# First stage of a two-layer streaming encoder: modulation pairs regrouped, the first projection chunks run between them, one pair moved, cache transposes split

## The chip, the cores and the metric

The kernel runs on one core of a Trainium2 chip. The metric is the device time of one execution, in microseconds (us); smaller is better. PE is TensorE, DVE is VectorE, ACT is ScalarE, POOL is GpSimd, and SP is the engine whose queue issues most of the transfers from HBM.

## The reference

Two streams of frames (256 prompt frames, 64 frames of a running stream, side by side as 320 columns) pass through two layers of width 1024. What matters here is the beginning of a layer:

```
c_act = silu(c)
mod = c_act @ w_ada[l] + b_ada[l]                 # (1024) @ (1024, 6144)
shift_m, scale_m, gate_m, shift_f, scale_f, gate_f = split(mod, 6)
h = rmsnorm(x, g_norm_mix[l]) * (1 + scale_m) + shift_m
q, k, v, iq, ik, iw, glu, sc, gates = split(h @ w_in[l], offsets)
```

k and ik (64 columns each) are the attention keys and the indexer keys. The running stream has 512 cached keys, values and indexer keys and two short histories for convolutions; they are joined to the new ones. Sparse attention, a 31-tap convolution on `glu`, a 3-tap convolution on `sc`, gated merging, an output projection and a feed-forward part (dense in layer 0, eight experts in layer 1) follow. All of it is float32.

## The kernel before

Activations lie transposed: 1024 channels are 8 blocks of 128 partitions by 320 columns (`xT`, `hT`). Every engine has one program, written out by hand, and they meet at counting semaphores; each engine works in its own order, and so does each transfer queue.

**Weights** come through `ring`, four slots of 1 MB, numbered in one sequence by `plan()`. `load(n)` on SP waits until chunk n - 4 has been computed (`chunk_done`), so the order of numbers is the order on SP and on PE. `ring_lo` and `hT_lo` lie in the same memory as `ring` and `hT`: the low part is written in place over the value.

**Modulation.** The 6144 columns of `w_ada` are cut into 12 pairs of ring units, 512 columns each (`ADA_COLS`); a unit holds half of the 1024 rows. `ada_pair` multiplies (64 small matmuls), ACT copies the sum to `modrow` (`ada_evac`), PE transposes it (`ada_turn`), DVE (`mods_add`) or ACT (`mods_bias`) adds the bias and counts `mods_added`. In layer 0 the pairs 0 to 3 (`ADA_FIRST`) give shift_m and scale_m: pair 0 and 1 the eight blocks of the shift, pair 2 and 3 those of the scale. Pair 4 belongs to the gate.

**Norm.** ACT squares x, `norm_sums` adds over channels on PE with a matrix of ones, ACT takes the root (`norm_std`), DVE the reciprocal (`norm_stats`); `norm_apply` on DVE and `norm_scale` on ACT make `hT` block by block (`h_ready`). Then `hT_hi` (ACT, rounded) and `hT_lo` (DVE, the difference) are made.

**Order on PE at the start of layer 0:** transposes of x; pairs 0 and 1; `norm_sums(0)`; turns of 0 to 3 with pairs 2 and 3 between them; two plain float32 chunks for K and indexer K (`pair_chunk("qkv", l, 0)` and `1`, weights in ring slots, each loaded twice side by side to fill 128 columns); pair 4; and then the 27 split chunks of `SPLIT`, of which the first are glu 0, glu 1, qkv 2, qkv 4 (v and indexer weights, 72 columns), qkv 3. A split chunk is three matmuls for each pair of blocks: high weight by high h, high weight by low h, low weight by high h. ACT makes the high part of a chunk's weights in two halves (`mix_high(s, r)`) and DVE the low part (`mix_low(s, r)`), both two chunks ahead: in its step s ACT does `mix_high(s + 2, 0)`, which waits until the load has landed, then the evacuation of chunk s, then `mix_high(s + 2, 1)`. The code between the two halves of a chunk on PE is the function `between`.

**Caches.** SP issues 14 small transfers (`cache_loads`) behind the load of glu 1. Behind chunk 2 (`S_CACHE`) PE turns them in seven batches through three banks of PSUM (`cache_transposes`), and DVE copies each out (`cache_copies`, counting `cache_copied`); the fourth batch can start only when the first is copied. POOL waits for all seven before it forms `u_conf`, which the convolution taps on DVE (`conv_taps`, dealt out over the steps by `TAPS_AT`) read. In the middle of chunk 4 (`S_KV`) PE turns the keys (`kv_transposes`), and waits there for `cache_copied` 7:

```
pe.wait_ge(mods_added, ADA_PAIRS * l + ADA_AT_QKV[l][1] + 1)
if l == 0:
    pe.wait_ge(cache_copied, 7)
pe.wait_ge(pair_evac, pair_no["qkv", l, 4] + 1)
```

The order on DVE in a step s is `mix_low(s + 2, 0)`, taps, `mix_low(s + 2, 1)`, `cache_copies` where it has its place, taps.

Of the kernel before, what the change touches and what calls it, by code (L numbers as in the profile page):

```python
# [27 lines left out]
P = 128  # L28
# [60 lines left out]
ADA_AT_QKV = ({1: 4}, {1: 6})  # L89
# [26 lines left out]
def plan():  # L116
# [17 lines left out]
    for l in range(DEPTH):  # L134
        for j in range(2):
            chunk("qkv", l, j)
            if j in ADA_AT_QKV[l]:
                ada(l, ADA_AT_QKV[l][j])
        for s, (stage, j) in enumerate(SPLIT[:NPROJ]):
            chunk(stage, l, j)  # L140
            if s in ADA_AT_SPLIT[l]:
                for h in range(2):
                    side[l, 2 * ADA_AT_SPLIT[l][s] + h] = len(side)
# [23 lines left out]
def build(nc, x_prompt, x_sample, cache_k, cache_v, cache_idx_k, state_conv_conformer, state_conv_short,  # L167
# [6 lines left out]
    with ExitStack() as ctx:  # L174
# [185 lines left out]

        sq_mix = wide[:, 0:DC, :]
# [44 lines left out]
        x_loaded = sem("x_loaded")  # L406
        caches_loaded = sem("caches_loaded")
# [165 lines left out]
        def _(sp):  # L573
# [26 lines left out]
            def ada_loads(l, m):  # L600
                for h in range(2):
                    parts = halves(ada_rows(l, 2 * m + h),
                                   w3["ada"][l][:, 4 * h:4 * h + 4, ADA_COLS * m:ADA_COLS * (m + 1)], 4)
# [13 lines left out]
            for m in range(ADA_FIRST):  # L617
                ada_loads(0, m)

# [11 lines left out]
            for l in range(DEPTH):  # L631
                win = w3["in"][l]
                for i, c in enumerate((K0, IK0)):
                    n = ring_no["qkv", l, i]
                    v = slot_view(n % SLOTS, DC, P)
                    load(n, [(v[:, :, r * HD:(r + 1) * HD], win[:, :, c:c + HD]) for r in range(2)])
                    if i in ADA_AT_QKV[l]:
                        ada_loads(l, ADA_AT_QKV[l][i])
# [4 lines left out]
                for s, (stage, j) in enumerate(SPLIT[:NPROJ]):  # L643
# [13 lines left out]
                    else:  # L657
# [3 lines left out]
                        if l and j == 8:  # L661
                            sp.wait_ge(mods_added, DEPTH * ADA_PAIRS)
                            for s_ in range(2):
                                for c in range(DC):
                                    sp.dma_start(gate_dram[s_, c * P:(c + 1) * P].unsqueeze(1),
                                                 mods[:, l, 40 + c, s_:s_ + 1]).then_inc(gate_stored, 16)
                    if s == 1 and l == 0:
# [90 lines left out]
        def _(pool):  # L758
# [14 lines left out]
            for l in range(DEPTH):  # L773

                pool.wait_ge(cache_copied, 7)
# [47 lines left out]
        def _(pe):  # L823
# [133 lines left out]
            def cache_transposes():  # L957
# [3 lines left out]
                for n in range(7):  # L961
                    b = (lg[:, 0:512], lg[:, 512:1024], px)[n % 3]
                    if n >= 3:
# [16 lines left out]

            pe.wait_ge(c_ready, 1)
            ada_pair(0, 0)
            ada_pair(0, 1)
            norm_sums(0)
            for m in range(ADA_FIRST):
                ada_turn(0, m)
                if m + 2 < ADA_FIRST:
                    ada_pair(0, m + 2)


            for l in range(DEPTH):
# [4 lines left out]
                pair_chunk("qkv", l, 0, h_rhs, blocks=((0, P),), width=P, each=h_each(2 * l))  # L996
                pair_chunk("qkv", l, 1, h_rhs, blocks=((0, P),), width=P)
# [1352 lines left out]
```

## Time and profile before

| | |
|---|---|
| median of 3 runs | 1468.35 us (1465.03 to 1468.79) |
| the profiled execution, its own time | 1463.33 us |
| its span in the trace | 1461.6 us |
| PE busy | 1391.8 us, 95% of the span |
| DVE busy | 1023.0 us, 70% |
| ACT busy | 781.2 us, 53% |
| POOL busy | 42.1 us, 3% |
| mean granted clock of PE | 0.981 of full speed |

The span is what the trace shows from the first to the last instruction; 1.7 us of the execution's time lie around it. A granted clock of 1.00 is 2.4 GHz, one of 0.50 is 1.2 GHz. The three runs differ among themselves by 3.8 us, and the profiled execution was faster than all of them.

### The profile page before, as it was taken

The page shows a single profiled execution, that of the slowest core. Times are in us where ns is not written, and L with a number is a line of the kernel's source. Part 1 is how long each engine was busy: PE and PEld are TensorE (multiplying, and loading weights), DVE is VectorE, ACT ScalarE, POOL GpSimd, SP SyncE. Part 2 cuts the span into 40 slices and gives each one's busy share as a digit, 9 for nine tenths or more (in the row PEclk, how much of TensorE's full clock was granted, in tenths as well). Part 3 has the DMA queues.
Part 4 walks back from the last instruction along what each step waited for, and adds up shares of the span by engine and source line. Part 5 has one row for each costly group of instructions (what it writes and reads, how often), then busy time and mean ns, then how long its engine had stood idle before and what let it go on. Part 6 is the DMA issues. An engine that isn't in the chain of part 4 may idle for free.

```text
span 1461.6 us, 24398 instructions
## 1 busy us (share of the span) xinstructions
PE 1391.8 (95%) x9311; PEld 1227.0 (84%) x9311; DVE 1023.0 (70%) x1401; ACT 781.2 (53%) x1058; POOL 42.1 (3%) x66
## 2 busy tenths in 40 slices
PE   5899999999889999997999999999799999999996
PEld 4788999877789999996989998778488888888884
DVE  2376999875554444235678998754788988898886
ACT  2534448634433333224444486344677887788763
POOL 0010100000000000000001000000200000000010
PEclk8999999999989999999999999999899999999999
DMA  9956744224546867543667764244689999999993
GB/s 305 244 165 194 258 133 131 73 72 149 167 137 195 259 201 238 200 129 96 209 202 252 213 139 151 73 136 159 247 303 386 386 381 384 376 386 386 377 381 115
DMA packets 282691, 328.40 MB, mean 225 GB/s; under 512 B 34654, under 2 KB 192806, under 8 KB 282598
## 3 DMA queue, kind: packets, MB, share of 16 engines
q1 hardware_dynamic: 276146, 317.18, 66.1%
q0 software_dynamic: 1472, 5.24, 1.0%
q10 hardware_dynamic: 4980, 4.69, 0.9%
q8 instruction: 63, 1.03, 0.3%
q14 instruction: 30, 0.25, 0.1%
HBM read 312.41 MB, written 14.66 MB: 224 GB/s over the span
## 4 chain that ended last, share of the span: by engine, by line
PE 89%; DVE 4%; DMA 3%; ACT 2%; SPq 1%; issue 1%; POOLq 0%; POOL 0%; DVEq 0%; ACTq 0%
PE mmp L856 14%; PE mmp L858 14%; PE mmp L857 14%; PE mmp L1258 8%; PE mmp L1260 8%; PE mmp L1259 8%; PE mmp L850 8%; PE py L826 2%; PE px L906 2%; DMA ring<-in_w_ada_dram 2%; PE lg L1022 1%; PE px L1064 1%; PE lg L906 1%; PE py L922 1%; DMA y_late<-rows_dram,pos_i 1%
## 5 line engine op out<-in xcount | busy, mean ns | idle before, releaser
L856 PE MATMUL mmp<-hT_hi,wm_hi 128*128 128x320 f32 (+1 forms) x976 | 306.7, 314 | 6.5 <-issue 4.9
L858 PE MATMUL mmp<-hT_hi,ring_lo 128*128 128x320 f32 (+1 forms) x976 | 304.3, 312 | 0.0
L857 PE MATMUL mmp<-hT_lo,wm_hi 128*128 128x320 f32 (+1 forms) x848 | 262.7, 310 | 0.0
L1867 DVE TENSOR_TENSOR ring_lo<-ring,wm_hi 128x1024 fp32r<-128x1024 f32 (+1 forms) x124 | 148.3, 1200 | 79.7 <-ACT wm_hi L1456 76.0
L856 PEld LDWEIGHTS mmp<-hT_hi,wm_hi 128*128 128x128 f32 (+1 forms) x976 | 183.1, 188 | 11.0 <-issue 7.3
L858 PEld LDWEIGHTS mmp<-hT_hi,ring_lo 128*128 128x128 f32 (+1 forms) x976 | 182.8, 187 | 0.2
L1456 ACT CAST wm_hi<-ring 128x1024 fp32r<-128x1024 f32 (+1 forms) x124 | 126.7, 1029 | 94.5 <-PE mmp L858 71.5
L857 PEld LDWEIGHTS mmp<-hT_lo,wm_hi 128*128 128x128 f32 (+1 forms) x848 | 159.0, 187 | 0.1
L1413 ACT ACTIVATE tmp<-mmp 128x320 f32<-128x320 f32 x70 | 30.6, 438 | 215.7 <-PE mmp L858 163.4
L1955 DVE SCALAR_TENSOR_TENSOR conv<-u_conf,dwc,conv 128x350 f32<-128x350 f32 x240 | 132.1, 581 | 3.0
L2089 DVE TENSOR_TENSOR wd_lo<-ring,wd_hi 128x2048 fp32r<-128x2048 f32 (+1 forms) x34 | 75.7, 2229 | 64.0 <-ACT wd_hi L1621 63.8
L856 PE MATMUL mmp<-h_hi,wd_hi 128*128 128x320 f32 x352 | 111.4, 316 | 8.8 <-DVE h_lo L2113 8.8
L857 PE MATMUL mmp<-h_lo,wd_hi 128*128 128x320 f32 x352 | 109.9, 312 | 0.0
L858 PE MATMUL mmp<-h_hi,wd_lo 128*128 128x320 f32 x352 | 109.9, 312 | 0.0
L2159 DVE TENSOR_TENSOR more_lo<-more,we_hi_a 128x2048 fp32r<-128x2048 f32 (+1 forms) x48 | 92.1, 1934 | 21.8 <-ACT we_hi_a L1674 19.0
L1258 PE MATMUL mmp<-we_hi_a,xg_hi 128*128 128x512 f32 (+1 forms) x256 | 98.4, 384 | 2.4 <-DVE xg_lo L2221 2.4
L2159 DVE TENSOR_TENSOR more_lo<-more,we_hi_b 128x2048 fp32r<-128x2048 f32 (+2 forms) x48 | 92.0, 1930 | 8.6 <-ACT we_hi_b L1674 8.6
L1260 PE MATMUL mmp<-we_hi_a,xg_lo 128*128 128x512 f32 (+1 forms) x256 | 97.2, 380 | 0.0
L2159 DVE TENSOR_TENSOR ring_lo<-ring,we_hi_a 128x2048 fp32r<-128x2048 f32 (+2 forms) x48 | 91.8, 1930 | 7.0 <-ACT we_hi_a L1674 6.9
L1621 ACT CAST wd_hi<-ring 128x2048 fp32r<-128x2048 f32 (+1 forms) x34 | 62.9, 1852 | 56.9 <-PE mmp L858 29.3
L1674 ACT CAST we_hi_a<-ring 128x2048 fp32r<-128x2048 f32 (+2 forms) x48 | 77.1, 1620 | 20.0 <-PE mmp L1260 15.5
L1674 ACT CAST we_hi_b<-more 128x2048 fp32r<-128x2048 f32 (+2 forms) x48 | 77.7, 1619 | 8.9 <-ACT y L1741 4.4
(389 smaller groups left out, 2851.8 us busy)
## 6 DMA issues: line engine op xcount, KB each, us to landing
ring<-in_w_in_dram SPq DMA_DIRECT2D x104, 512.0 KB, 4.9
ring<-in_w_exp_in_dram SPq DMA_DIRECT2D x64, 512.0 KB, 8.5
more<-in_w_exp_in_dram SPq DMA_DIRECT2D x64, 512.0 KB, 11.3
ring<-in_w_ada_dram SPq DMA_DIRECT2D x56, 512.0 KB, 6.8
more<-in_w_exp_out_dram SPq DMA_DIRECT2D x48, 512.0 KB, 6.1
ring<-in_w_ffn_in_dram SPq DMA_DIRECT2D x44, 512.0 KB, 5.8
wide<-in_w_ada_dram SPq DMA_DIRECT2D x40, 512.0 KB, 7.6
ring<-in_w_branch_dram SPq DMA_DIRECT2D x48, 256.0 KB, 2.9
```

Of the source, the lines that this page charges most:

```text
L850: ins = nc.tensor.matmul(mmp[0:m, 2 * (q % 2) + b, 0:T], v[:, i, c0:c0 + m], rhs(i), start=(i == 0), stop=(i == k - 1))
L856: nc.tensor.matmul(out, w_hi, x_hi, start=is_first, stop=False)
L857: nc.tensor.matmul(out, w_hi, x_lo, start=False, stop=False)
L858: return nc.tensor.matmul(out, w_lo, x_hi, start=False, stop=is_last)
L1258: nc.tensor.matmul(bank, x_hi, w_hi, start=is_first, stop=False)
L1259: nc.tensor.matmul(bank, x_hi, w_lo, start=False, stop=False)
L1260: return nc.tensor.matmul(bank, x_lo, w_hi, start=False, stop=is_last)
L1456: copy(mix_hi(l, s, r), mix_rows(ring, l, s, r)).then_inc(mix_hi_ready, 1)
L1674: copy(we_hi(k)[:, 0:sizes[kk]], we_raw(k)[:, 0:sizes[kk]]).then_inc(hi_ready, 1)
L1867: V.tensor_tensor(mix_rows(ring_lo, l, s, r), mix_rows(ring, l, s, r), mix_hi(l, s, r).bitcast(F32), ALU.subtract).then_inc(mix_lo_ready, 1)
L1955: ins = V.scalar_tensor_tensor(conv[:, c, :], src, tap, conv[:, c, :], ALU.mult, ALU.add)
L2159: V.tensor_tensor(we_lo(k)[:, 0:size], we_raw(k)[:, 0:size], we_hi(k)[:, 0:size].bitcast(F32), ALU.subtract).then_inc(lo_ready, 1)
```

## The change

Layer 0 alone changes, apart from renamed constants.

- **Pairs 0 to 3** now hold two blocks of shift and the two matching blocks of scale each. Their transfers read two stretches of 256 columns (rows of 1 KB) where they read one of 512 (rows of 2 KB). `mods_add` becomes two additions, `gains` and `norm_apply` run for two blocks after each pair.
- **PE** does `norm_sums(0)` first, then each pair with its turn at once behind it, and after each of the turns 1, 2, 3 and once more at the end the K and indexer K products of two blocks of h (`keys_first`).
- **K weights** no longer use the ring. They are loaded once, into the unused `merged`, between pair 1 and pair 2 on SP's queue, and ACT doubles them side by side.
- **ACT** scales two blocks of h after each pair and rounds them; **DVE** makes the low parts as soon as `keys_first` has read a block.
- **Pair 4** is loaded and computed behind glu 1; its turn stands in the middle of qkv 2.
- **Cache transposes and copies** come in two portions: batches 0 to 2 behind chunk 2, batches 3 to 6 behind chunk 3, the last through another bank. POOL waits for three in layer 0.

```diff
-ADA_AT_QKV = ({1: 4}, {1: 6})
+ADA_AT_QKV = (4, 6)
+ADA_BEHIND = (1, None)
...
-        ring[stage, l, j], pair[stage, l, j] = n, q
-        n, q = n + 1, q + 1
+        pair[stage, l, j] = q
+        q += 1
+        if (stage, l) != ("qkv", 0) or j >= 2:
+            ring[stage, l, j] = n
+            n += 1
...
         for s, (stage, j) in enumerate(SPLIT[:NPROJ]):
             chunk(stage, l, j)
+            if s == ADA_BEHIND[l]:
+                ada(l, ADA_AT_QKV[l])
...
+                    v, src = ada_rows(l, 2 * m + h), w3["ada"][l][:, 4 * h:4 * h + 4, :]
+                    if m < ADA_FIRST:
+                        parts = [(v[:, :, 2 * P * r:2 * P * (r + 1)],
+                                  src[:, :, D * r + 2 * P * m:D * r + 2 * P * (m + 1)]) for r in range(2)]
...
             for m in range(ADA_FIRST):
                 ada_loads(0, m)
+                if m == 1:
+                    for i, c in enumerate((K0, IK0)):
+                        sp.dma_start(wk0[:, i, :, 0:HD], w3["in"][0][:, :, c:c + HD]).then_inc(k_loaded, 16)
...
+                    if s == ADA_BEHIND[l]:
+                        ada_loads(l, ADA_AT_QKV[l])
                     if s == 1 and l == 0:
                         cache_loads()
...
-                pool.wait_ge(cache_copied, 7)
+                pool.wait_ge(cache_copied, (3, 7)[l])
...
+            def keys_first(m):
+
+                if m == 0:
+                    pe.wait_ge(k_doubled, 2)
+                for c in range(2 * m, 2 * m + 2):
+                    pe.wait_ge(h_ready, c + 1)
+                    for j in range(2):
+                        ins = nc.tensor.matmul(mmp[:, 2 * (pair_no["qkv", 0, j] % 2), 0:T], wk0[:, j, c, :], hT[:, c, :],
+                                               start=(c == 0), stop=(c == DC - 1))
+                ins.then_inc(k_done, 1)
+
+            norm_sums(0)
             pe.wait_ge(c_ready, 1)
             ada_pair(0, 0)
+            ada_turn(0, 0)
             ada_pair(0, 1)
-            norm_sums(0)
+            ada_turn(0, 1)
             for m in range(ADA_FIRST):
-                ada_turn(0, m)
+                keys_first(m)
                 if m + 2 < ADA_FIRST:
                     ada_pair(0, m + 2)
+                    ada_turn(0, m + 2)
...
                     def between():
+                        if ADA_BEHIND[l] is not None and s - 1 == ADA_BEHIND[l]:
+                            ada_turn(l, ADA_AT_QKV[l])
...
+                    if s == ADA_BEHIND[l]:
+                        ada_pair(l, ADA_AT_QKV[l])
                     if s == S_CACHE and l == 0:
-                        pe.wait_ge(mods_added, ADA_AT_QKV[0][1] + 1)
-                        cache_transposes()
+                        pe.wait_ge(mods_added, ADA_AT_QKV[0] + 1)
+                        cache_transposes(range(3))
+                    if s == S_CACHE + 1 and l == 0:
+                        cache_transposes(range(3, 7))
...
                     norm_std(0)
-                    for m in range(2, ADA_FIRST):
+                    for m in range(ADA_FIRST):
                         ada_evac(0, m)
-                    norm_scale(0, gain_of(0), shift_of(0))
+                        if m == 1:
+                            act.wait_ge(k_loaded, 32)
+                            for j in range(2):
+                                copy(wk0[:, j, :, HD:P], wk0[:, j, :, 0:HD]).then_inc(k_doubled, 1)
+                        if m >= 1:
+                            norm_scale(0, gain_of(0), shift_of(0), range(2 * m - 2, 2 * m))
+                            high_h(range(2 * m - 2, 2 * m))
+                    norm_scale(0, gain_of(0), shift_of(0), range(DC - 2, DC))
+                    high_h(range(DC - 2, DC))
...
+                if l == 0:
+                    mix_high(0, 0)
...
+                    if ADA_BEHIND[l] is not None and s - 1 == ADA_BEHIND[l]:
+                        mods_bias(l, ADA_AT_QKV[l])
...
+                    if s == ADA_BEHIND[l]:
+                        ada_evac(l, ADA_AT_QKV[l])
...
                     for m in range(ADA_FIRST):
                         mods_add(0, m)
-                    gains(0, 0)
-                norm_apply(2 * l)
+                        gains(0, 0, 2 * m, 2 * m + 2)
+                        norm_apply(0, 2 * m, 2 * m + 2)
+                        if m == ADA_FIRST - 2:
+                            hT_lows(range(DC // 2))
...
                     if s == S_CACHE and l == 0:
-                        cache_copies()
+                        cache_copies(range(3))
+                    if s == S_CACHE + 1 and l == 0:
+                        cache_copies(range(3, 7))
```

## Rows read from the trace of the kernel before

**Rows 1.** The page, part 1: busy us, share of the span, instructions.

```profile
PE 1391.8 (95%) x9311; PEld 1227.0 (84%) x9311; DVE 1023.0 (70%) x1401; ACT 781.2 (53%) x1058; POOL 42.1 (3%) x66
```

**Rows 2.** Timeline of PE, 0 to 80 us: start us, us, instructions, idle before.

```profile
14.18 0.63 PE L941 MATMUL mmp<-ident,wide 96*128 96x96 f32 x2 [2.64 <-DMA wide<-in_w_dw_conf_dram]
...
20.29 4.57 PE L922 MATMUL py<-wide,ones 128*128 128x320 f32 x16
...
24.91 1.95 PE L906 MATMUL px<-ring,c 128*32 128x128 f32 x64
...
33.39 0.48 PE L915 MATMUL lg<-ident,modrow 128*128 128x128 f32 x1
36.54 11.13 PE L850 MATMUL mmp<-hT,ring 128*128 128x320 f32 x32 [2.67 <-ACT hT L1389]
...
52.61 0.39 PE L856 MATMUL mmp<-hT_hi,wm_hi 128*128 128x320 f32 x1 [3.06 <-issue]
...
75.51 1.03 PE L972 MATMUL lg<-ident,wide 128*128 128x128 f32 x8
```

**Rows 3.** Timeline of DVE and ACT before K.

```profile
25.54 2.15 DVE L1831 RECIPROCAL rstd<-std 128x320 f32<-128x320 f32 x1 [10.11 <-ACT std L1382]
...
35.79 4.84 ACT L1389 ACTIVATE hT<-hT,mods,gain 128x256 f32<-128x256 f32 x8 [2.45 <-DVE hT L1843]
```

**Rows 4.** Windows of 1 us: length, PE busy, granted clock, DMA share, GB/s.

```profile
13.00:14.00 1.00, 0.00 (x0) 0.92 1.04 333
...
17.00:18.00 1.00, 1.00 (x40) 0.87 1.03 332
...
23.00:24.00 1.00, 1.00 (x5) 1.00 0.99 365
...
31.00:32.00 1.00, 0.98 (x20) 0.50 1.33 220
...
69.00:70.00 1.00, 1.00 (x9) 1.00 1.09 382
...
79.00:80.00 1.00, 0.45 (x2) 0.50 1.19 298
...
85.00:86.00 1.00, 1.00 (x7) 0.74 0.00 0
```

**Rows 5.** Timeline of SP's queue.

```profile
43.40 5.30 SPq L588 DMA_DIRECT2D ring<-in_w_in_dram  x4
...
58.51 30.16 SPq L588 DMA_DIRECT2D ring<-in_w_in_dram  x12
```

**Rows 6.** Landing of the transfers issued from 59.6 us (qkv 4).

```profile
DMA to landing us min/median/max: 6.5/6.8/7.1
```

**Rows 7.** Landing of one issued at 75.7 us with nothing ahead.

```profile
DMA to landing us min/median/max: 4.0/4.0/4.0
```

**Rows 8.** Waits, 0 to 110 us: total, times, longest.

```profile
PE mmp L856 <- ACTq L1416: 1.3, 1, 1.3
...
PE lg L972 <- DVE kTs L1809: 2.4, 1, 2.4
```

**Rows 9.** Timeline of DVE, 45 to 150 us.

```profile
78.81 0.68 DVE L1809 COPY kTs<-lg 128x512 f32<-128x512 f32 x1
...
80.01 0.28 DVE L1811 COPY hist<-px 128x128 f32<-128x128 f32 x1
...
83.34 0.29 DVE L1807 COPY dwc<-lg 128x124 f32<-128x124 f32 x1
85.37 1.01 DVE L1952 TENSOR_SCALAR conv<-u_conf,dwc,vec 128x350 f32<-128x350 f32 x1 [1.74 <-POOL u_conf L788]
...
90.53 2.18 DVE L1955 SCALAR_TENSOR_TENSOR conv<-u_conf,dwc,conv 128x350 f32<-128x350 f32 x4
...
93.89 3.30 DVE L1955 SCALAR_TENSOR_TENSOR conv<-u_conf,dwc,conv 128x350 f32<-128x350 f32 x6
```

**Rows 10.** The chain that ended last: the key transposes in chunk 4.

```profile
91.24 0.57 PE lg L1009 x6
```

More of the change, by code:

```diff
@@ L633, in _ @@
                 for i, c in enumerate((K0, IK0)):
[L634 to L638, printed above, removed]
+                    if l:
+                        n = ring_no["qkv", l, i]
+                        v = slot_view(n % SLOTS, DC, P)
+                        load(n, [(v[:, :, r * HD:(r + 1) * HD], win[:, :, c:c + HD]) for r in range(2)])
+                if ADA_BEHIND[l] is None:
+                    ada_loads(l, ADA_AT_QKV[l])
                 def clear_rows(b):
@@ L1383, in norm_std, with norm_scale @@
                                      bias=eps[:, 0:1]).then_inc(std_ready, 1)
-            def norm_scale(k, gain_of, shift_of):
-                for c in range(DC):
+            def norm_scale(k, gain_of, shift_of, blocks=range(DC)):
+                for c in blocks:
                     act.wait_ge(xn_ready, DC * k + c + 1)
@@ L1423, in shift_of, with high_h @@
                     return lambda c: mods[:, l, 24 * which + c, 0:1]
+                def high_h(blocks):
+                    for c in blocks:
+                        act.wait_ge(h_ready, DC * 2 * l + c + 1)
+                        copy(hT_hi[:, c, :], hT[:, c, :]).then_inc(hT_hi_ready, 1)
                 if l == 0:
@@ L1436, in _ @@
                     norm(2 * l, gain_of(0), shift_of(0))
[L1439 to L1446 removed]
+                    high_h(range(DC))
                 def mix_high(s, r):
@@ L1456, in mix_high @@
                     copy(mix_hi(l, s, r), mix_rows(ring, l, s, r)).then_inc(mix_hi_ready, 1)
-                for r in range(2):
+                if l == 0:
+                    mix_high(0, 0)
+                for j, (dst, dst_s) in enumerate(((kT, kTs), (ikT, ikTs))):
+                    if l:
+                        chunk_wait(ring_no["qkv", l, j])
+                    else:
+                        act.wait_ge(k_done, ADA_FIRST)
+                    copy(dst[:, 0:T], pair("qkv", l, j, 0))
+                    copy(dst[:, T:TW], pair("qkv", l, j, 0)[:, TP:T])
+                    copy(dst_s[:, l, PAST:NKS], pair("qkv", l, j, 0)[:, TP:T]).then_inc(pair_evac, 1)
+                for r in range(2) if l else (1,):
                     mix_high(0, r)
-                ada_evac(l, ADA_AT_QKV[l][1])
+                if ADA_BEHIND[l] is None:
+                    ada_evac(l, ADA_AT_QKV[l])
                 for r in range(2):
@@ L1798, in _, with cache_copies @@
             link(V.tensor_copy(dwc[:, 0, :], mmp[:, b % 4, P:P + CW * BC]))
-            def cache_copies():
-                for n in range(7):
-                    s = (lg[:, 0:512], lg[:, 512:1024], px)[n % 3]
+            def cache_copies(batches):
+                for n in batches:
+                    s = (lg[:, 0:512], lg[:, 512:1024], px)[n % 3] if n < 6 else py
                     l, what = n // 3, n % 3
```

119 lines of the change are left out of this document (70 added, 49 removed).

## The prediction

> **What bounds the kernel now.** The page first: PE is busy for 1391.8 of 1461.6 us [rows 1]. A change pays only where it shortens PE's own way through the program. Next the granted clock in windows of 1 us, because everything here happens in the first 91 us, where PE has pauses: it falls to half in the pause before 14 us, is back at 17.9, is at half again from 31 to about 41, and once more from 79 to 85.7 [rows 4]. Then the timelines. PE starts glu 0, the first split chunk, at 52.61, the transposes of the caches at 75.51, and the key transposes in the middle of chunk 4 at 91.24 [rows 2, 10]. From there PE has no gap, and nothing behind it is changed. So the question is only when PE reaches the key transposes, and at what clock. I call these times G (start of glu 0), E (end of qkv 2) and V (key transposes): before, G = 52.6, E = 75.5, V = 91.2.
>
> **G, the part that gains.** I follow the new order from the last unchanged moment, the small transposes at 14.18 [rows 2], which end at 14.8.
>
> - The channel sums come first: 4.57 us at full clock [rows 2]. The clock is half until 17.9 [rows 4], so 3.1 us do 1.6 us of the work, and the sums end at 20.9.
> - Pair 0 takes 1.95 us [rows 2] to 22.8. Now its turn follows at once. Pair 3's turn starts at 33.39, 0.4 us after its last matmul (1.94 us from 31.02), for ACT's copy between. So each pair with its turn costs 1.95 + 0.4 + 0.3 = 2.65, and pair 1 is turned at 25.8. The reciprocal of 2.15 us [rows 3] lies beside this.
> - The first products of K need both doublings of the weights (my estimate 0.6 us each, between ACT's 0.43 us for 320 columns and 1.05 for 1024) and one scaled block (eight in 4.84 us, and PE starts 0.75 after the first begins [rows 2, 3]): 25.2 + 0.3 + 1.2 + 0.75 = 27.5.
> - The 32 matmuls of K took 11.13 us partly at half clock [rows 2]; at full clock one starts each 0.27 us, eight are 2.15 us. From 27.5: K 29.7; pair 2 has landed by 30.1 and is done at 31.5, turned at 32.2; K again needs a block scaled after pair 2's copy, 32.6 to 34.8; pair 3 to 36.7, turn 37.4; K 37.8 to 40.0, and 40.0 to 42.1.
> - Landing: a unit of 1.05 MB takes 2.9 us at 365 GB/s [rows 4]. K's 0.5 MB, in rows of 256 bytes, goes at 220 GB/s [rows 4], 2.4 us, ahead of pair 2. And pair 2's load waits until pair 0 is computed, now 5 us later than before, so the queue runs dry for some 2 us. First unit free at 21.8, then 5.5 to land, then 2.9 each: 27.3, 30.2, 33.1, 36.0. PE asks for the last at 35.75: no more than 0.3 us is lost.
> - Then ACT's cast and DVE's difference for glu 0 (1.05 and 1.23 us) start at 41.3, behind the rounding of the last block. glu 0's weights are there: their slot is free at 30.6. Before, their load was issued at 43.40 [rows 5], and PE's start hung on it. G = 43.7.
>
> With one fall of the clock after the pause of 25.8 to 27.5 (before, pauses like it cost the clock at 14 and at 31, but a longer one at 50 did not) some 4.5 us run at half, 2.2 us of loss. At an even chance that is 1.1. G = 44.8, **7.8 us earlier**. Bounds: 41 (below) and 48 (two falls).
>
> **G to E, the part that gives back.** Three chunks take 75.51 - 52.61 less the 1.3 us of waiting for ACT [rows 2, 8]: 7.2 each. Now pair 4 stands between glu 1 and qkv 2: +1.95. The wait of 1.3 goes (qkv 2's load was issued at 58.51, behind the cache transfers [rows 5]; now it goes out at G + 7.3, lands by G + 12.3, and ACT frees the bank by G + 15.5, before PE needs it at 16.4).
>
> But the turn of pair 4 stands in the middle of qkv 2, at G + 14.4 + 1.95 + 3.6 = G + 19.95, and needs ACT's `ada_evac`, which stands behind `mix_high(3, 0)`, the evacuation of glu 1 and `mix_high(3, 1)`. `mix_high(3, 0)` waits for the load of qkv 4. That load takes the slot of glu 1, so it is issued at G + 14.5, two transfers 0.5 apart; from issue to landing they took 6.5 to 7.1 us behind other transfers [rows 6], and one with nothing ahead took 4.0 [rows 7]. I take 5.3: landed at G + 20.3. ACT then needs 2.0 us for the four steps (read from the same steps at 69.97 to 71.95). The turn is at G + 22.4, PE has stood for 2.4 us (1.1 with 4.0, 4.2 with 7.1), and qkv 2 ends at 22.4 + 0.3 + 3.6 = G + 26.3. Before it was G + 22.9: **+3.4**. A pause of that length may take the clock; at an even chance half of 3.6 us, **+0.9**. qkv 3's load is queued behind qkv 4's, ACT's bias for pair 4 behind the cast of qkv 3, and PE asks for that bias before the transposes: 0 to 1.5, I take **+0.5**.
>
> **E to V, the split of the caches.** It takes away PE's wait of 2.4 us for the fourth batch [rows 8]; the half clock that follows on it (to 85.7) goes too. On PE alone E to V would shrink from 15.7 to about 10.2: 1.2 for three batches, 3.6 for chunk 3, 1.8 for four batches, 3.6 for half of chunk 4. But PE still waits for `cache_copied` 7 there, and on DVE the last four copies now stand behind step 3's taps and `mix_low(5, 1)`. DVE's chain from E: the first copy began 3.3 after E [rows 2, 9] (evacuation, cast, difference); three copies 1.5, to the end of the third [rows 9]; POOL's `u_conf`, which DVE waited 1.74 for [rows 9]; six taps, `mix_low(5, 0)`, four taps, `mix_low(5, 1)`: 93.89 - 85.37 = 8.5 [rows 9]; four copies, 1.5 for three and 0.5 for the two small ones; 0.1 for the semaphore. 3.3 + 1.5 + 1.7 + 8.5 + 2.0 + 0.1 = 17.1, where it was 15.7: **+1.4**. PE stands for about 7 us in the middle of chunk 4. Before, it had got back its full clock at 85.7, ahead of V; now the clock has certainly fallen and comes back 3.7 (from 14.2) to 6.1 us (from 79.6) after PE resumes [rows 4], a loss of half: 1.8 to 3.0, I take **+2.3**. Behind V DVE is ahead by its six taps, which nobody waits for; the first side load, which waits for the seven transposes, is earlier by more than it needs.
>
> **Nothing for** the second addition in `mods_add` and the gains in four portions (0.2 us each, beside PE's pairs), SP's 14 cache issues (9.8 us, now in glu 0's shadow; without that cover qkv 2's load would slip by up to 6), and the last batch in another bank.
>
> **Rows of 1 KB.** The first pairs are read in rows half as long. In this trace such rows, those of qkv 3, moved at 382 GB/s, the present 2 KB rows at 365 [rows 4]: no cost. The Trainium skill ("DMA: Bandwidth & Descriptors", Why small descriptors are slow) puts a fixed 3 cycles on every packet beside one for each 32 bytes, 35 for 32 against 67 for 64, which would be 4.5% on 8.4 MB, an estimate of 1.0 us later at the last pair. By that rule the sum would be up to 1 us higher; by the rows it is not.
>
> **The sum**: -7.8 + 3.4 + 0.9 + 0.5 + 1.4 + 2.3 = +0.7 us. Against the profiled execution: 1463.3 + 0.7 = 1464.0. That execution lies 5.0 below the median, so the median would be 1469.0.
>
> **Rivals.**
> 1. *The early stage runs at full clock.* If w_dw_conf's rows, for which PE stood until 14.18 [rows 2], arrive with the first squares (13.1), the clock does not fall, the sums end at about 16.5, pair 2 is loaded without a dry queue, and G is 41.0 to 41.5 by the transfers alone (9.7 MB at 365 GB/s and K's 2.4 us, less 2.8 at the last pair). With no fall after it and the short landing of qkv 4: -3.6 - 1.3 - 0.9 more, a sum of about -5, 1463. For it: 1 KB rows leave the other queue more often a turn. Against: the sums and squares are unchanged, and 333 GB/s flowed without pause. The Trainium skill (same page, Queues, rings and completion order) has engines change queues at whole packets, of several rows each; if so, shorter rows give the small transfers nothing, and this rival loses its ground.
> 2. *The chain on DVE does not bind.* If PE walks through E to V at its own 10.2 us, the last two terms become -5.5 and 0: -8.5, 1460. For it only that four copies are 2 us of work. It decides if the copies are done by E + 10; the order on DVE says E + 17.
> 3. *Slower: half clock between the pairs.* PE's work from 27.5 to 42.1 is 12.5 us in short pieces with pauses for ACT between. If the clock stays at half there, as it did from 31 to 41 [rows 4], these are 25, of which pauses and landings cover 3 to 4: G near 53, sum +9, 1477. From 10 us at half clock on it is slower by more than 0.3%. For it: before, the same stage did run so. Against: PE was idle for half of it, now for a fifth.
>
> **Chances.** 0.3% is 4.4 us, about what runs of this kernel (3.8 us apart) can tell from no change. The forecast, within that: 0.58. Rival 1: 0.15, rival 2: 0.07, both faster, 0.22. Rival 3 and its milder forms: 0.20. The range leaves out rival 2 and the upper part of rival 3: from -7.4 to +6.7, 1461 to 1475.
>
> **What would show it.** G at 43 to 46. PE waiting at its turn in the middle of qkv 2 for ACT, 1 to 4 us. DVE's last four copies behind the difference of chunk 5, and PE idle some 7 us before the key transposes, which start at about 89, then half clock for 4 to 6 us. It is wrong if the key transposes start before 85, if PE does not stand there, or if K's products run at 0.53 us each.

## The result and the profile after

The changed kernel takes 1470.86 us (median of 20 runs, 1465.68 to 1476.26) against 1466.02 for the kernel before in the same comparison (20 runs, 1460.58 to 1474.29). The ratio is 1.0024, 95% interval 1.0013 to 1.0034: 3.5 us slower, between 1.9 and 5.0. (The ratio is that of the means; the medians lie 4.8 us apart.) The 3.5 us are inside the 0.3% which the prediction called no change, near its upper edge. A second comparison (12 and 23 runs) gave 1.0036 [1.0015, 1.0058]. The forecast was 1469.0 us and +0.7. It starts from a median of 1468.3 for the kernel before, where this comparison has 1466.0, so the +0.7 is the number to judge: its sign is right and its size too small.

| profiled execution | before | after |
|---|---|---|
| own time, us | 1463.33 | 1466.45 |
| span, us | 1461.6 | 1464.7 |
| G, start of glu 0 | 52.61 | 45.01 |
| E, end of qkv 2 | 75.51 | 72.30 |
| V, key transposes | 91.08 | 89.40 |
| S, first scores of the attention | 95.60 | 96.73 |

(V of before is the start on PE's timeline. The chain of [rows 10] enters that group at 91.24, the moment from which the prediction counted its 15.7.) I add S, the first matmul of `lg<-prob,iqT`, because part of the price of a pause is paid behind V.

The page after, part 1, answers to [rows 1]:

```profile
PE 1394.1 (95%) x9311; PEld 1227.3 (84%) x9311; DVE 1025.3 (70%) x1415; ACT 782.1 (53%) x1060; POOL 44.3 (3%) x66
```

PE does the same number of matmuls and is busy 2.3 us longer: the added time is not all waiting, some of it is work at a lower clock.

**The early stage.** Timeline of PE of the changed kernel, 12 to 64 us, beside [rows 2]:

```profile
13.08 0.41 PE L968 MATMUL mmp<-ident,wide 96*128 96x96 f32 x2 [1.88 <-DMA wide<-in_w_dw_conf_dram]
13.33 6.16 PE L949 MATMUL py<-wide,ones 128*128 128x320 f32 x16
19.42 1.95 PE L933 MATMUL lg<-ring,c 128*32 128x128 f32 x64
...
26.09 3.52 PE L1015 MATMUL mmp<-hT,merged 128*128 128x320 f32 x8 [1.30 <-ACT hT L1437]
...
32.93 2.42 PE L1015 MATMUL mmp<-hT,merged 128*128 128x320 f32 x8 [0.17 <-ACT hT L1437]
...
37.09 1.08 PE L933 MATMUL lg<-ring,c 128*32 128x128 f32 x32 [0.72 <-DMA ring<-in_w_ada_dram]
...
39.10 4.88 PE L1015 MATMUL mmp<-hT,merged 128*128 128x320 f32 x16 [0.17 <-ACT hT L1437]
45.01 0.39 PE L883 MATMUL mmp<-hT_hi,wm_hi 128*128 128x320 f32 x1 [1.04 <-ACT kTs L1517]
...
59.26 1.95 PE L933 MATMUL px<-ring,c 128*32 128x128 f32 x64
63.51 0.42 PE L883 MATMUL mmp<-hT_hi,wm_hi 128*128 128x320 f32 x1 [2.30 <-ACTq L1464]
```

Each line can be laid beside the walk in the prediction. A pair with its turn takes 2.65 us, as forecast (the next pair starts at 22.07). The first eight products of K are slow, 3.52 us, and the next eight take their 2.42 us at full clock. The wait of 1.04 before glu 0 is put down to ACT's copy of the keys, but that was done at 44.67. What PE waited for longest is DVE's difference for glu 0, which ends at 44.91, as the prediction had it.

**The clock in that stage**, windows of 1 us of the changed kernel. The columns are length, busy us (and instructions) of PE, PEld, DVE, ACT and POOL, then the granted clock, the DMA share and GB/s:

```profile
13.00:14.00 1.00, 0.92 (x4) 0.78 (x5) 0.44 (x2) 1.00 (x3) 0.00 (x0) 0.78 1.10 346
16.00:17.00 1.00, 1.00 (x3) 0.61 (x3) 0.00 (x0) 0.00 (x0) 0.00 (x0) 0.52 1.11 351
21.00:22.00 1.00, 0.56 (x17) 0.24 (x5) 1.00 (x1) 0.27 (x1) 0.00 (x0) 1.00 0.50 110
27.00:28.00 1.00, 1.00 (x4) 0.70 (x3) 0.00 (x0) 0.15 (x1) 0.00 (x0) 0.60 1.05 368
```

The clock fell at about 13.6, and once more behind the pause at 26, to half from about 27.2 to 30.6; then no more before glu 0. In [rows 4] the kernel before ran at half here from 31 to 41. The queue ran dry at 21 to 22 us (110 GB/s), as forecast.

**The caches.** Timeline of DVE of the changed kernel, 74 to 92 us, beside [rows 9]:

```profile
74.46 1.22 DVE L1958 TENSOR_TENSOR ring_lo<-ring,wm_hi 128x1024 fp32r<-128x1024 f32 x1 [3.23 <-ACT wm_hi L1506]
75.60 0.68 DVE L1875 COPY kTs<-lg 128x512 f32<-128x512 f32 x1
...
76.80 0.28 DVE L1877 COPY hist<-px 128x128 f32<-128x128 f32 x1
78.82 1.00 DVE L2040 TENSOR_SCALAR conv<-u_conf,dwc,vec 128x350 f32<-128x350 f32 x1 [1.74 <-POOL u_conf L815]
...
80.61 2.19 DVE L2043 SCALAR_TENSOR_TENSOR conv<-u_conf,dwc,conv 128x350 f32<-128x350 f32 x4
82.83 1.23 DVE L1958 TENSOR_TENSOR ring_lo<-ring,wm_hi 128x1024 fp32r<-128x1024 f32 x1
83.97 2.18 DVE L2043 SCALAR_TENSOR_TENSOR conv<-u_conf,dwc,conv 128x350 f32<-128x350 f32 x4
86.19 1.23 DVE L1958 TENSOR_TENSOR ring_lo<-ring,wm_hi 128x1024 fp32r<-128x1024 f32 x1
87.33 0.69 DVE L1875 COPY kTs<-lg 128x512 f32<-128x512 f32 x1
...
89.01 0.29 DVE L1873 COPY dwc<-py 128x124 f32<-128x124 f32 x1
```

And what PE does meanwhile, in the chain that ended last:

```profile
77.57 0.87 PE lg L999 x8
82.90 6.50 issue
89.40 1.33 PE lg L1051 x6
```

The transposes of the fourth batch begin on PE at about 77.4 (the chain joins them at 77.57), and their copy on DVE at 87.33, ten us later, because the four copies, 2 us together, stand behind ten taps and two differences. "Issue" is the name for a wait that the profile connects with nothing; the releaser is the last copy, which ends 0.1 us before PE's first key transpose. The clock beside it:

```profile
85.00:86.00 1.00, 0.00 (x0) 0.00 (x0) 0.96 (x3) 0.00 (x0) 0.00 (x0) 0.62 1.06 403
...
95.00:96.00 1.00, 1.00 (x7) 1.00 (x6) 0.96 (x3) 0.00 (x0) 0.00 (x0) 0.76 0.38 82
```

It falls in the pause (0.62 in the slice from 85, so at about 85.2, 2.3 us after PE stopped) and is back at 95.5, 6.1 us after PE resumed. From V to S it takes 7.3 us, before 4.5.

### The profile page after: what moved, and what is told of

It is laid out like the page before. It is cut to its first block, busy times and chain, and to the rows that moved or that the text cites. A ratio compares the mean times of both kernels' runs of the same rounds, so it can differ in the third digit from the quotient of the medians.

```text
span 1464.7 us, 24425 instructions
## 1 busy us (share of the span) xinstructions
PE 1394.1 (95%) x9311; PEld 1227.3 (84%) x9311; DVE 1025.3 (70%) x1415; ACT 782.1 (53%) x1060; POOL 44.3 (3%) x66
## 4 chain that ended last, share of the span: by engine, by line
PE 87%; DVE 4%; DMA 2%; ACT 2%; SPq 2%; issue 1%; ACTq 0%; POOLq 0%; POOL 0%; DVEq 0%
PE mmp L883 13%; PE mmp L885 13%; PE mmp L884 13%; PE mmp L1306 8%; PE mmp L1308 8%; PE mmp L1307 8%; PE mmp L877 7%; PE px L933 2%; PE py L853 2%; DMA ring<-in_w_in_dram 1%; PE py L949 1%; PE lg L1064 1%; PE lg L933 1%; SPq L690 1%; PE px L1106 1%
## 5 line engine op out<-in xcount | busy, mean ns | idle before, releaser
L1461 ACT ACTIVATE tmp<-mmp 128x320 f32<-128x320 f32 x70 | 30.6, 437 | 213.9 <-PE mmp L885 161.7
L2179 DVE TENSOR_TENSOR wd_lo<-ring,wd_hi 128x2048 fp32r<-128x2048 f32 (+1 forms) x34 | 75.7, 2230 | 65.0 <-ACT wd_hi L1687 64.9
```

## The experiments

All results are ratios to the kernel before on the same chip, with 95% intervals, unless us are named. "In its trace" is one execution. First the two parts of the change were separated.

**One portion.** The changed kernel with caches turned and copied as before:

```diff
-                        cache_transposes(range(3))
-                    if s == S_CACHE + 1 and l == 0:
-                        cache_transposes(range(3, 7))
+                        cache_transposes(range(7))
```

and the same for `cache_copies`; POOL waits for seven again, and the last batch is in its old bank.

> The changed kernel with the cache transposes and copies in one portion again (seven batches behind chunk 2, POOL waiting for seven, the last batch in its old bank); all else as changed. My theory (what the split costs: DVE's last four copies lie behind ten taps, PE stands in the middle of chunk 4 and then runs at half clock): PE's wait of 6.5 us before the key transposes goes, one of about 2.4 us for the fourth batch returns, E to V is 15.7 us instead of 17.1, and the clock is full at V. That is 4 us less than the changed kernel, a ratio of 0.999 to 1.000 to the kernel before. Rival (the loss comes from somewhere else, the split costs nothing in the end): 1.002 to 1.003 as the changed kernel.

Measured: 0.999 [0.997, 1.001]. In its trace E to V is 14.6 (changed kernel 17.1) and V to S 4.5 (7.3). So everything but the split is worth 1.5 us of gain, with an interval from a gain of 4.4 to a loss of 1.5, and the split costs the changed kernel some 5 us (0.999 against 1.0024; from the two intervals, an estimate of 5 with 3 either way).

**The split alone.** The kernel before, with the two portions of the diff and nothing else of it.

> The kernel before with the split of the cache transposes and copies alone. My theory: E stays at 75.5, V comes at E + 17.1 = 92.6 instead of 91.2, PE stands some 6 us in the middle of chunk 4 and runs at half clock for some 5 us behind it: 1.4 + 2.9, slower by 4 us, a ratio of 1.002 to 1.004. Rival (the split does what it does on PE alone: it removes the wait of 2.4 us and the half clock that follows): V at 86 to 88, faster by 3 to 5 us, 0.997.

Measured: 1.0040 [1.0026, 1.0055], 5.9 us slower (3.8 to 8.1). In its trace E to V is 17.1, PE idles 6.50 us ahead of V, and V to S is 7.2. It is the same picture without any of the other edits:

```profile
90.30 6.50 issue
96.79 1.33 PE lg L1009 x6
```

**The four copies ahead of the taps.** The changed kernel, where DVE's order alone differs; PE's order stays (excerpt, as all edits here):

```diff
                     if s == S_CACHE and l == 0:
                         cache_copies(range(3))
-                    if s == S_CACHE + 1 and l == 0:
                         cache_copies(range(3, 7))
```

> The changed kernel, split kept on PE, but DVE does its last four cache copies right behind the first three, ahead of the six taps that end step 2. My theory: PE reaches the key transposes by its own work, about 10.2 us behind the end of qkv 2, without the wait of 6.5 us and without the half clock after it: 6.9 + 2.9 = 9.8 us less than the changed kernel, a ratio of 0.995 to 0.997 to the kernel before. Rival (the taps, now 1.5 us later, hold up the low parts of chunks 5 and 6, and PE waits there instead): PE idle at chunk 5 or 6, ratio 0.999 or more.

Measured: 0.9942 [0.9923, 0.9961], median 1459.89, more gain than the 0.995 to 0.997 expected: this one and "both", below, are the fastest kernels here. Timeline of DVE in its trace:

```profile
76.83 0.69 DVE L1875 COPY kTs<-lg 128x512 f32<-128x512 f32 x1 [0.97 <-PE lg L999]
...
78.52 0.29 DVE L1873 COPY dwc<-py 128x124 f32<-128x124 f32 x1
78.72 0.83 DVE L2040 TENSOR_SCALAR conv<-u_conf,dwc,vec 128x350 f32<-128x350 f32 x2
```

DVE waits 0.97 us for PE instead of 1.74 for POOL, and PE does not stand anywhere from E to V: 10.5 us, the "own 10.2" of the prediction. V is at 81.53 and S at 86.05. One line of order is worth 12 us (0.9942 against 1.0024).

**The four copies at the head of step 3**, behind step 2's taps only:

```diff
+                    if s == S_CACHE + 1 and l == 0:
+                        cache_copies(range(3, 7))
                     if s + 2 < NPROJ:
                         mix_low(s + 2, 0)
...
-                    if s == S_CACHE + 1 and l == 0:
-                        cache_copies(range(3, 7))
```

> The changed kernel, DVE's last four cache copies at the beginning of its step 3: behind the six taps that end step 2, ahead of the low part of chunk 5 and the four taps. A dose between the changed kernel (V at E + 17.1) and copies ahead of all taps (E + 10.3). My theory, the order on DVE alone: V at E + 12.6, PE waits about 2.4 us before the key transposes, too short to be sure that the clock falls: 4.5 to 7.4 us less than the changed kernel, a ratio of 0.996 to 0.999 to the kernel before. Rival (any pause there costs the clock, the place matters little): 0.999 to 1.001.

Measured: 0.9988 [0.9972, 1.0003]. E to V is 12.6, and V to S is 4.5. In the chain of its trace:

```profile
82.37 1.99 issue
84.36 0.76 PE lg L1051 x6
```

In this trace a pause of 2 us costs its 2 us and no clock; the one of 6.5 costs 2.2 to 2.8 more behind it in every trace that has it.

**The kernel before with the split, copies ahead of the taps.**

> The kernel before with the split of the cache transposes, and DVE's last four copies right behind the first three, ahead of the taps; nothing regrouped. My theory: the split done in this order removes the wait of 2.4 us for the fourth batch and the half clock that follows it: V at E + 10.4 instead of E + 15.6, 5 us less than the kernel before, a ratio of 0.996 to 0.998. If so, more than half of the gain of the changed kernel with this order (0.9942) comes from the caches and less than half from the pairs. Rival (the pause only moves, as it did in the changed kernel): 0.999 or more.

Measured: 0.9983 [0.9960, 1.0006], less gain than the expected 0.996 to 0.998. E to V is 10.4, as expected. With the split alone it was 1.0040, so the place of the four copies is worth 8.4 us in this kernel. Of the 8.5 us that the changed kernel gains with this order, 2.5 come from the caches (0.9983) and 6.0 from the rest of the change (0.9983 against 0.9942, some 4 us either way by the two intervals); more than half from the caches was expected.

**Pair 4 at the front**, behind pair 3 as before, in the changed kernel: `ADA_BEHIND = (None, None)`.

> The changed kernel with pair 4 loaded and computed in front of glu 0 again, split kept. My theory: G is 1.5 to 2.5 us later, but qkv 2's slot is free before glu 0 starts and the cache transfers are issued earlier, so PE waits neither at the start of qkv 2 nor at a turn in its middle: three chunks in 21.6 us instead of 27.3. E 3 to 4 us earlier, V at E + 17.1 as before: about 4 us less than the changed kernel, 0.9985 to 1.001 to the kernel before. Rival (moving pair 4 is worth its 1.95 us: it leaves the way to G and costs nothing behind): slower than the changed kernel, 1.003 or more.

Measured: 1.0016 [0.9997, 1.0036], outside the expected 0.9985 to 1.001. G moves to 48.8 and E stays, 72.2 against 72.3; G to E is 23.4 where 21.6 was expected. The start of glu 0 in PE's timeline:

```profile
48.81 0.39 PE L883 MATMUL mmp<-hT_hi,wm_hi 128*128 128x320 f32 x1 [2.24 <-ACT ikTs L1517]
```

Another 1.81 us go at the start of qkv 2. In front, PE waits 2.24 + 1.81 us at the two starts; with the pair behind glu 1 it is 1.04 + 2.30. E is 72.2 and 72.0 in the two traces with the pair in front, and 71.7 on the mean of the six with it behind and the caches on SP's queue: the place of the pair makes no difference that these runs can show.

**Regrouped pairs alone**: one portion and pair 4 in front.

> The regrouped pairs with K between them alone: caches in one portion, pair 4 in front of glu 0, as in the kernel before. My theory: G at 46 to 47 (52.6 before), E at G + 21.6 = 68, V at E + 15.7 = 84, full clock at V: 7 us earlier than before, a ratio of 0.994 to 0.997. Rival (the gain at G is lost again in E to V, or by half clock between the pairs, whatever the other parts do): 0.998 or more.

Measured: 0.9988 [0.9972, 1.0004], less gain than the expected 0.994 to 0.997. In its trace the clock fell around pair 3 (its second half took 1.93 us where 1.08 is usual), G was 49.4 and S 92.3, 3.3 ahead of the kernel before. With the caches in one portion the fourth batch waits 2.42 us again, and E to V is 15.8. The lead at S is there, and 1.8 us of it are in the time.

**Cache transfers on ACT's queue.** In the changed kernel the cost of SP's 14 issues was under suspicion (next section). They go out on ACT's queue behind `row_loads(1)`; the loop over the caches is the same, with `act.dma_start` for `sp.dma_start`.

> The changed kernel with the 14 cache transfers issued from ACT's queue behind the bias rows of layer 1, not from SP's ahead of qkv 2. In the changed kernel qkv 2's load is issued at 54.77 behind them, 2.7 us after glu 0 has ended. My theory: the load goes out at about 52.3, PE's wait of 2.3 us at the start of qkv 2 goes, but the turn of pair 4 in its middle waits for ACT instead, 0.5 to 2 us; E is 1 to 3 us earlier and everything behind it, as E to V stays 17.1: 1 to 4 us less than the changed kernel, 0.9995 to 1.002 to the kernel before. Rival (small transfers on a second queue slow qkv 2's load as much as the issues did): no difference, 1.0024.

Measured: 1.0032 [1.0016, 1.0047], where 0.9995 to 1.002 was expected. Its trace shows the mechanism that was expected: PE waits 0.92 us before qkv 2 and 0.47 at the turn, V is at 85.50 and S at 92.36, 4.4 earlier than in the changed kernel's first trace and 3.7 earlier than the mean of its three. On ACT's queue the 14 issues take 7.1 us. The time shows nothing of the lead: the mean granted clock is 0.9777 over its 12 runs and 0.9795 over the 29 of before beside them, and 0.0018 of the time is 2.6 us.

**Both: copies ahead and transfers on ACT's queue.**

> Two edits together on the changed kernel: DVE's last four cache copies ahead of the taps, and the cache transfers issued from ACT's queue. Alone they gave 0.9942 and 1.0032 to the kernel before. If the 4 us that the second one gained up to the key transposes in its trace are real and only lost in the scatter, this is 0.991 to 0.993. If ACT's issues give nothing in the end: 0.994 as the first alone.

Measured: 0.9943 [0.9924, 0.9963]. S is at 83.62, again 2.4 earlier than with the copies ahead alone, and again the time is the same. But the intervals of the two leave room for some 4 us either way, so this pair cannot tell 2.4 from nothing; the pair before it, with 4.4 us at S, is the one that speaks.

**Controls.** The changed kernel once more, timed; one more execution of the kernel before and one of the changed kernel, on the same chip.

> The changed kernel itself, once more beside the kernel before, on the chip of this call. It measures how much of the differences between my experiments is scatter between calls. Expected 1.001 to 1.004 (1.0024 so far), G at 44 to 46, V at E + 17.1. If the trace shows a fall of the clock near 885 and near 1050 us too, as seven of the eight experiments did and the two first traces did not, these falls belong to the chip or the execution and not to an edit.

> One look at the kernel before, for its trace alone. In the first trace the split chunks began at 52.6 us and the first scores at 95.6; with the same code up to there, the trace of the split alone began them at 55.8. Expected 52.5 to 56, and between 1366 and 1372 us from the first scores to the end. If it lies near 55.8, the first trace was an early one and the changed kernel's gain at G was larger than the 7.6 us that the two traces show.

> One look at the changed kernel, for its trace alone. Expected G at 44 to 46, the wait before the key transposes 6.5 us, and 1368 to 1376 us from the first scores to the end.

Measured: 1.0036 [1.0015, 1.0058] for the first; 1469.93 us for the one execution of before, 1475.06 for the last. Some expectations were missed at their edges: G of the changed kernel was 43.4 and 46.7 where 44 to 46 was expected, and span less S was 1377.0 in the last and 1372.8 in the control of before. The clock falls near 892 in both controls of the changed kernel, and in the control of before too. So that fall does not belong to an edit. The table sets the marks of all traces side by side:

| trace | G | E | V | S | span | span less S |
|---|---|---|---|---|---|---|
| before | 52.6 | 75.5 | 91.1 | 95.6 | 1461.6 | 1366.0 |
| before, control | 53.3 | 76.2 | 90.8 | 95.3 | 1468.1 | 1372.8 |
| changed | 45.0 | 72.3 | 89.4 | 96.7 | 1464.7 | 1368.0 |
| changed, control 1 | 43.4 | 70.8 | 87.9 | 95.0 | 1471.8 | 1376.8 |
| changed, control 2 | 46.7 | 72.5 | 89.6 | 96.3 | 1473.3 | 1377.0 |
| one portion | 44.4 | 71.9 | 86.5 | 91.0 | 1467.1 | 1376.1 |
| copies ahead | 43.6 | 71.1 | 81.5 | 86.1 | 1459.1 | 1373.0 |
| copies at head of step 3 | 44.3 | 71.8 | 84.4 | 88.9 | 1462.0 | 1373.1 |
| pair 4 in front | 48.8 | 72.2 | 89.3 | 96.4 | 1470.2 | 1373.8 |
| regrouped alone | 49.4 | 72.0 | 87.8 | 92.3 | 1467.4 | 1375.1 |
| caches on ACT | 43.3 | 68.4 | 85.5 | 92.4 | 1465.4 | 1373.0 |
| both | 43.7 | 68.7 | 79.1 | 83.6 | 1457.7 | 1374.1 |
| split alone | 55.8 | 79.7 | 96.8 | 104.0 | 1474.8 | 1370.8 |
| split, copies ahead | 53.1 | 76.1 | 86.6 | 91.1 | 1467.0 | 1375.9 |

## Why the prediction held, point by point

**G: right, 45.0 against 44.8.** The terms were nearly all as worked out. Three small errors cancel, so that the hit to 0.2 us is in part luck. The rows of `w_dw_conf` arrived 1.1 us earlier than assumed (13.08 against 14.18 in [rows 2]), which was the condition of rival 1. That is not chance: it is 13.1 to 13.5 in all ten traces with the new pairs and 14.1 to 14.3 in all four without; the runs do not separate the shorter rows from the new order of the loads as the cause. Nor does the prediction's second argument against the rival follow from its own premise: if queues change at whole packets of several rows each, shorter rows make shorter packets, and the small transfers get their turn sooner. In this execution the clock fell at about 13.6 all the same (0.78 in that slice). In five of the other nine the sums took 4.5 to 4.6 us, their time at full clock, as the rival had it; there the clock fell behind the pause at 25 instead, and G was 43.3 to 44.3. The rival's 41.0 to 41.5 came in none. K's matmuls take 0.30 us each at full clock and not 0.27. And 0.7 us went to the last unit of pair 3, where 0.3 was the bound. Rival 3 is out: the pauses of 0.4 us for ACT between the pairs did not hold the clock down. A milder form of it exists: the trace with the regrouped pairs alone had a second fall, at pair 3. Over the three traces of the changed kernel G is 43.4 to 46.7. The latest has the longest channel sums: they take 7.23 us, one starting each 0.53 us up to about 19, as at half clock. The column of the granted clock reads 1.00 in all of this time. Here is its row, and that of the first control, whose sums take 4.57:

```profile
14.00:15.00 1.00, 1.00 (x3) 0.61 (x3) 0.54 (x2) 1.00 (x2) 0.00 (x0) 1.00 1.09 344
```

```profile
14.00:15.00 1.00, 1.00 (x6) 0.68 (x5) 0.24 (x1) 1.00 (x3) 0.00 (x0) 1.00 1.10 347
```

So in the first 20 us the column does not show every slow stretch, and the length of single matmuls must be read beside it.

**G to E: right in size, wrong in place.** 27.3 us were measured where the prediction had 26.3 + 0.9 + 0.5 = 27.7, against 22.9 before. But the wait was forecast at the turn of pair 4 in the middle of qkv 2, and there PE did not stand. It stood 2.30 us at the start of qkv 2, the very wait that the forecast had removed. The step that failed is the one that put SP's 14 cache issues "in glu 0's shadow". SP's queue in the changed kernel:

```profile
38.59 3.45 SPq L605 DMA_DIRECT2D ring<-in_w_ada_dram  x4
42.07 1.93 SPq L649 DMA_DIRECT2D wide<-in_cache_k_dram  x2
...
54.34 0.39 SPq L652 DMA_DIRECT2D cv<-in_cache_v_dram  x1
54.77 9.59 SPq L605 DMA_DIRECT2D ring<-in_w_in_dram  x8
```

Pair 4's load now stands behind glu 1's on that queue, and the caches behind pair 4's: they start at 42.07, not with glu 0, and take 12.7 us, not 9.8. qkv 2's load goes out at 54.77, 2.7 us after its slot was free (glu 0 ends at 52.05). The prediction had priced that slip, "up to 6 without that cover", and said that the cover was there. The chain of waits that follows:

```profile
55.32 4.95 DMA ring<-in_w_in_dram
60.30 1.05 ACT wm_hi L1506
...
61.69 1.28 ACT L1462
62.98 0.45 ACT tmp L1462
```

ACT's cast waits for the load, and the evacuation of glu 0 stands behind the cast with a table load of 1.28 us in it; PE needs the bank that it frees. Having stood there, PE reached the turn late enough to find ACT ready. The clock was at half from about 64.8 to 68.2, the forecast's even chance; it kept full in the second control, where G to E is 25.8. With the issues taken off SP the wait shrinks to 0.92 and the turn waits 0.47, which shows that SP's issues caused most of it. Its time shows no gain from that, which stays unexplained (below).

**E to V: right, 17.1 us to the tenth.** The chain on DVE was summed from the rows of before, and each item came as priced. Rival 2 is out: the copies were done 17.0 after E, where 10 was its point of decision. Two experiments with the DVE order alone settle the cause: 17.1, 12.6 and 10.5 us for the three places of the four copies.

**The size of the split was too small.** The prediction had +1.4 and +2.3, 3.7 together. Measured it is 5.0 (one portion to changed) and 5.9 (before to split alone); 3.7 lies inside the interval of the first and just below that of the second (3.8 to 8.1). Both terms look a little small. The half clock behind V costs 2.2 to 2.8 (6.8 to 7.3 from V to S in the six traces that have the pause, 4.5 in all others). And 15.7 us from E to V [rows 2, 10] was the long variant of before: with the caches in one portion the clock falls at the wait of 2.4 us [rows 8] for a longer or a shorter stretch: the control and the one-portion kernel take 14.6, the regrouped pairs alone 15.8. So E to V costs 2.0 against the mean of the two traces of before, and 1.9 against the two with the new pairs (2.5 and 1.3). With 2.6 behind V, the mean of the three traces of the changed kernel, that gives 4.5 to 4.6, inside both intervals.

**The sum.** Up to E the regrouping gains 4.0 us (mean of three traces 71.9, of two 75.8; forecast 3.0), the split gives 4.6 back, and S is 0.6 later (means 96.0 and 95.4). What is measured at the end is 3.5 [1.9, 5.0]. Some 3 us therefore arise behind S, where the two programs are the same. So the forecast of +0.7 was met at S, with the gain and the price each about 1 us larger than forecast. The prediction said "from there PE has no gap, and nothing behind it is changed": this is the step that fell short. The column "span less S" shows where it goes. The window from 700 to 1100 us, in the first trace of before and in its control:

```profile
700.00:1100.00 400.00, 385.87 (x2562) 331.87 (x2560) 305.85 (x529) 215.01 (x348) 17.97 (x20) 0.99 0.60 192
```

```profile
700.00:1100.00 400.00, 385.97 (x2541) 331.51 (x2540) 301.12 (x526) 210.82 (x346) 18.19 (x20) 0.97 0.59 186
```

The clock of this stretch, the third number from the end of the row, is 0.99 in the first trace of before and of the changed kernel, and 0.97 in the control of before, as in both controls of the changed kernel. Summed over windows of 1 us from 100 us to the end, the time short of full clock (length times one less the clock) is 17.0 and 23.9 us in the two traces of before, and 18.7, 28.2 and 28.8 in the three of the changed kernel. Against the first trace these are 6.9, 1.6, 11.2 and 11.8 more; "span less S" is longer by 6.8, 2.0, 10.8 and 11.0. Over all fourteen traces, "span less S" less that shortfall is 1346.8 to 1350.1 us, but for one of 1352.1 (one portion). So what arises behind S is the clock, in every kernel. Whether the changed kernel loses more of it is not shown. The shortfall is 17.0 to 28.6 in the four traces with the early stage of before and 18.7 to 28.8 in the ten with the new one. The runs point that way: in the second comparison the mean granted clock was 0.9797 over 23 runs of before and 0.9771 over 12 of the changed kernel; 0.0026 of 1470 us is 3.8 us. The first 100 us do not explain it: in their windows the column falls short by 10.2 us in both traces of before, and by 10.2, 8.5 and 3.4 in those of the changed kernel (it misses some 3 us in the last, by the long sums above). I could not isolate the cause: the kernels have the same instructions there, and no experiment took the clock away. For the same reason it is open why the caches on ACT's queue bring 4.4 us at S and nothing at the end.

**What the regrouping alone is worth** can be read from three pairs of kernels that differ in it, and in the place of pair 4: 1.5 us with the caches in one portion (1.0000 to 0.9990), 2.3 with them split (1.0040 to 1.0024), 6.0 with the copies ahead (0.9983 to 0.9942). The three agree within their intervals, of 3 to 4 us either way, and do not fix the size. At G and E the lead is better known from all traces with the same code up to there: G is 44.3 on the mean of eight and 53.7 of four, E 71.7 of six and 76.9 of four. So the lead is 9.4 us at G and 5.2 at E, where the first two traces gave 7.6 and 3.2.

**Rows of 1 KB.** The prediction counted no cost, by the 382 GB/s of qkv 3. In windows of 1 us at the same moments, first before, then changed:

```profile
8.00:9.00 1.00, 1.00 (x7) 1.00 (x6) 0.30 (x1) 0.08 (x2) 0.00 (x0) 1.00 1.07 386
16.00:17.00 1.00, 1.00 (x28) 0.90 (x21) 0.00 (x0) 0.00 (x0) 0.00 (x0) 0.50 1.05 385
```

```profile
8.00:9.00 1.00, 1.00 (x7) 1.00 (x6) 0.67 (x1) 0.18 (x2) 0.00 (x0) 1.00 1.12 350
```

At 16 us the changed kernel has 351, as shown above. These two moments are alike in all traces: 379 to 389 in the four with 2 KB rows, 343 to 351 in the ten with rows of 1 KB, 9 to 10% less. Both stages have other transfers among them, so this is no clean measurement, but it leans to the rule of the Trainium skill ("DMA: Bandwidth & Descriptors", Why small descriptors are slow) and against my row; the loss is about twice the 4.5% that the prediction worked out from the rule. What it cost is not known: G came 0.2 us behind the forecast, but with errors in it that cancel.

## What to carry to other kernels

When a wait of one engine is split in two, read the order of the engine that must release it: here PE's second half was ready at 77, and its four copies of 2 us stood behind ten convolution taps until 87. Moving them ahead of the taps turned a change of +3.5 us into one of -8.5.

A gain of 7.6 us early in the program was worth 3 to 5 at the next join, because the next wait was on another queue (SP's, with 14 small issues in front of the load), and at the end between 1.5 and 6, by three pairs of kernels. Mark a few fixed points of the bound engine in every trace and carry the difference from one to the next; a single difference of spans says less than the scatter of one execution.

## What the runs showed of the hardware

The scatter between executions of one program, 10 to 16 us here, is mostly the granted clock. The time and the mean clock of the runs of before have a correlation of -0.83, -0.85 and -0.74 in three comparisons (23, 29 and 31 runs). The same wait costs the clock in one execution and not in another, or costs it for longer. The wait of 2.3 to 2.5 us ahead of qkv 2 was followed by half clock in five of the six traces that have it, and not in the second control of the changed kernel. The wait of 2.42 us for the fourth cache batch was followed by some 6.8 us of half clock in the first trace of before and with the regrouped pairs alone, and by 3.4 in the control and in the one-portion kernel. A third place is not quite alike. Windows of 2 us of the first trace of before, and then of its control:

```profile
886.00:888.00 2.00, 1.93 (x18) 1.50 (x18) 1.97 (x4) 1.26 (x2) 0.00 (x0) 1.00 1.08 383
888.00:890.00 2.00, 0.58 (x6) 0.18 (x4) 1.72 (x5) 1.87 (x6) 0.00 (x0) 1.00 0.58 206
890.00:892.00 2.00, 2.00 (x16) 2.00 (x16) 2.00 (x3) 0.59 (x1) 0.00 (x0) 1.00 0.05 18
```

```profile
888.00:890.00 2.00, 0.70 (x4) 0.30 (x4) 1.72 (x5) 1.62 (x5) 0.00 (x0) 1.00 1.00 353
890.00:892.00 2.00, 1.48 (x8) 1.48 (x9) 2.00 (x3) 1.16 (x3) 0.00 (x0) 0.76 0.13 47
892.00:894.00 2.00, 2.00 (x9) 2.00 (x9) 1.93 (x5) 0.55 (x3) 0.00 (x0) 0.50 0.00 2
```

Both have a wait of 1.42 us for DVE; in the second one of 0.53 stands 1.2 us ahead of its start. In the first the clock stays at full, in the second PE works at half from about 891. The pause of 2 us with the copies at the head of step 3 kept the clock in its one trace, the one of 6.5 us lost it in all six traces that have it. In this kernel a forecast could take the pause of 6.5 us as certain to cost the clock and had to leave those near 2 us as a chance.

Small transfers are dear to the queue that issues them: 14 of them kept SP for 12.7 us in the changed kernel, and the load behind them went out 2.7 us late. What stands in front of them matters: with pair 4's load right ahead they took 12.7 to 13.1 us in six traces, with pair 4 in front of glu 0 they took 8.8 to 9.8 in six others.
